# A diffusion trunk's gated linear attention: scan levels grown from the level below, and half of the gate slabs computed with the input

## What is computed

```python
def gla_project(h, w_in, w_a1, w_a2, b_a):
    p = h @ w_in                      # q 512, k 512, v 1024, g 1024 columns
    ...
    low = jnp.einsum('btd,zdr->zbtr', h, w_a1)
    logits = jnp.einsum('zbtr,zrk->zbtk', low, w_a2) + b_a[:, None, None, :]
    log_decay = jax.nn.log_sigmoid(logits.astype(jnp.float32)) / GLA_GATE_NORM
    ...
def step(state, inp):                 # one chunk of tokens, one head
    qc, kc, vc, lc = inp
    cum = jnp.cumsum(lc, axis=2)
    rel = jnp.where(lower, cum[:, :, :, None, :] - cum[:, :, None, :, :], -jnp.inf)
    attn = jnp.einsum('bhtd,bhsd,bhtsd->bhts', qc, kc, jnp.exp(rel))
    last = cum[:, :, -1:, :]
    out = attn @ vc + jnp.einsum('bhtd,bhdv->bhtv', qc * jnp.exp(cum), state)
    state = (jnp.exp(last[:, :, 0, :, None]) * state
             + jnp.einsum('bhsd,bhsv->bhdv', kc * jnp.exp(last - cum), vc))
    return state, out
def gla_output(o, g, head_norm, w_out):
    o = from_heads(rms_norm(o, head_norm))
    return (o * jax.nn.silu(g)) @ w_out
```

## Time and profile before

| | us |
|---|---|
| median of 3 runs | 1734.85 (1732.74 to 1736.03) |
| the profiled execution, its own time | 1732.71 |
| its span, first to last instruction | 1730.9 |
| PE busy | 1661.2 (96%) |
| DVE busy | 1122.6 (65%) |
| ACT busy | 713.6 (41%) |
| POOL busy | 85.8 (5%) |

### The profile page before, as it was taken

The page is one execution under the profiler, slowest core; times in us unless marked ns, Lnnn a source line. Parts: engine busy times, 40 slices in busy tenths (PEclk is TensorE's granted clock), DMA queues, the critical chain, the costliest instruction groups (busy, mean ns, idle before and its releaser), DMA issues.

```text
span 1730.9 us, 23892 instructions
## 1 busy us (share of the span) xinstructions
PE 1661.2 (96%) x9008; PEld 1390.0 (80%) x9008; DVE 1122.6 (65%) x1816; ACT 713.6 (41%) x1060; POOL 85.8 (5%) x57
## 2 busy tenths in 40 slices
PE   7999999998999999999999899989989899999997
PEld 6888877887888888888888777866777688888885
DVE  6678666477877477865775555188855664464456
ACT  4222565336333233322334664256644543343345
POOL 0200000122000000000002200000002100000002
PEclk9999999999999999999999999999999999999999
DMA  8334100031434333334312121110112223333332
GB/s 359 121 141 160 48 1 1 25 134 37 147 101 142 134 109 131 112 134 136 119 62 76 37 64 59 36 35 25 37 62 86 72 94 96 96 95 97 96 97 73
DMA packets 37280, 159.51 MB, mean 92 GB/s; under 512 B 4145, under 2 KB 4401, under 8 KB 31057
## 3 DMA queue, kind: packets, MB, share of 16 engines
q1 hardware_dynamic: 37202, 158.44, 27.5%
HBM read 156.33 MB, written 2.10 MB: 92 GB/s over the span
## 4 chain that ended last, share of the span: by engine, by line
PE 84%; DVE 7%; ACT 5%; issue 2%; DMA 1%; POOL 0%; SPq 0%; ACTq 0%; DVEq 0%
PE pm L484 59%; PE pm L466 5%; PE pm L718 4%; PE pm L638 3%; PE pm L504 2%; PE pm L664 2%; PE pm L897 2%; PE pm L651 1%; ACT mod_t L983 1%; DMA ada_w<-first_ada 1%; DVE h_res L1658 1%; PE pm L840 1%; PE pm L595 1%; PE pm L551 1%; PE pm L822 1%
## 5 line engine op out<-in xcount | busy, mean ns | idle before, releaser
L1382 DVE TENSOR_TENSOR w_lo<-raw,w_hi 128x1024 fp32r<-128x1024 f32 x185 | 230.8, 1249 | 367.0 <-ACT w_hi L964 364.5
L964 ACT ACTIVATE w_hi<-raw 128x1024 fp32r<-128x1024 f32 x181 | 191.8, 1060 | 631.2 <-PE pm L484 535.0
L484 PE MATMUL pm<-x_hi,w_hi 128*128 128x512 f32 (+1 forms) x1464 | 428.8, 354 | 0.7 <-DVE w_lo L1382 0.7
L484 PE MATMUL pm<-x_hi,w_lo 128*128 128x512 f32 (+1 forms) x1464 | 424.0, 351 | 0.0
L484 PE MATMUL pm<-x_lo,w_hi 128*128 128x512 f32 (+1 forms) x1464 | 423.4, 350 | 0.0
L484 PEld LDWEIGHTS pm<-x_lo,w_hi 128*128 128x128 f32 x1464 | 237.8, 189 | 40.6
L484 PEld LDWEIGHTS pm<-x_hi,w_hi 128*128 128x128 f32 x1464 | 237.1, 189 | 39.5 <-issue 1.0
L484 PEld LDWEIGHTS pm<-x_hi,w_lo 128*128 128x128 f32 x1464 | 235.6, 188 | 39.0
L1408 DVE CUSTOM_DVE_ANT_0 ada_w<-ada_w,cond_rep 128x1024 f32<-128x1024 f32 x80 | 102.6, 1282 | 0.0
L484 PE MATMUL pm<-hid_hi,w_hi 128*128 128x512 f32 x330 | 100.6, 359 | 0.2 <-DVE w_lo L1382 0.2
L484 PE MATMUL pm<-hid_lo,w_hi 128*128 128x512 f32 x330 | 99.3, 355 | 0.0
(11 more groups left out here) (242 smaller groups left out, 2525.9 us busy)
## 6 DMA issues: line engine op xcount, KB each, us to landing
raw<-slabs SPq DMA_DIRECT2D x185, 512.0 KB, 3.6
ada_w<-ada SPq DMA_DIRECT2D x44, 1024.0 KB, 4.9
ada_w<-first_ada SPq DMA_DIRECT2D x4, 1024.0 KB, 19.0
raw<-gates SPq DMA_DIRECT2D x8, 512.0 KB, 3.6
h_res<-x SPq DMA_DIRECT2D x4, 768.0 KB, 17.0
out<-h_res SPq DMA_DIRECT2D x8, 256.0 KB, 2.0
rope<-rope SPq DMA_DIRECT2D x1, 512.0 KB, 23.2
level_f<-level SPq DMA_DIRECT2D x1, 448.0 KB, 3.3
```

The lines of the kernel that those rows point to most:

```text
L484: last = pe.matmul(out_p[:, a:b], w[slot][:, ks], x[:, k, a:b], start=(k == 0 and w is w_hi and x is hi), stop=(k == tiles - 1 and w is w_lo))
L964: act.activation(w_hi[nxt % 2][:, :], raw[nxt % 4][:, :], ACT.Copy).then_inc(sem["split_hi"], 1)
L1382: dve.tensor_tensor(w_lo[nxt % 2][:, :], raw[nxt % 4][:, :], w_hi[nxt % 2][:, :].bitcast(FP32), ALU.subtract).then_inc(sem["split_lo"], 1)
```

## The change

1. **Levels grown.** VectorE's step_raw(h) takes the differences of cum from token to token, ScalarE's step_decay(h) their exponential: fold0. GpSimd, which had nothing in the scan, multiplies neighbours: fold1 to fold6, the decay over blocks of 2 to 64 tokens. Keys and queries then grow from level to level: what is faded to its block's middle is multiplied by the neighbouring block's factor, 512 of 1,024 elements each (grow_keys, grow_queries on VectorE, in place in the tile faded). ScalarE's merge_keys copies both halves of the keys into key_sides, which has two buffers; the queries are read by TensorE from faded itself, by an access pattern. Level 1 needs only set_queries. The last factor gives the queries for the states (fade_queries, keep_queries) in place of an exponential per direction.
2. **Gates.** Four slabs of g (the even ones) become ordinary split slabs between the queries and the values (S_GLA_G, take_gate); the other four stay in the scan, one per head, with a new GATE_STEPS: one tile on most steps.
3. **Order in the input.** The last pair of logits and decays goes behind slab 8 instead of 7, for n in (0, 2, 4, 7). The decay exponentials of the chunk sums go ahead of the value slabs.
4. SP waits for q_done as well before it loads over the folds' buffer. The sums of the two directions change places in cum.

The core of the diff:

```diff
         GATE_STEPS = {}
         for h in range(GLA_HEADS):
-            spans = ((0, 3), (3, 6), (6, 8), (8, 11), (11, 13), (13, 15), (15, 16)) if h < GLA_HEADS - 1 else (
-                (0, 4), (4, 8), (8, 11), (11, 14), (14, 16))
-            for b, (k, end) in enumerate(spans):
-                i = 2 * h + k // KT
-                GATE_STEPS[GLA_LEVELS * h + b] = (i, k % KT, (end - 1) % KT + 1)
+            ends = (4, 5, 5, 6, 6, 7, 8) if h == 0 else (2, 3, 4, 5, 6, 7, 8) if h < GLA_HEADS - 1 else (2, 4, 6, 7, 8)
+            for b, (k, end) in enumerate(zip((0,) + ends, ends)):
+                GATE_STEPS[GLA_LEVELS * h + b] = (h, k, end)
...
+        def key_side(h, lv, c):
+
+            if lv <= 1:
+                return gla_k[:, h, c * P:(c + 1) * P]
+            return key_sides[:, lv % 2, c * P:(c + 1) * P]
+
+        def query_side(h, lv, c):
+
+            if lv == 0:
+                return gla_q[:, h, c * P:(c + 1) * P]
+            m = 1 << lv - 1
+            v = faded[:, 0, c * P:(c + 1) * P]
+            return bass.AP(v.tensor, v.offset, [v.ap[0], [2 * m, P // (2 * m)], [3 * LAT + m, 2], [1, m]])
...
-        def segments(b, z, h, src=None):
+        def growing(b, slots, right):
 
             m = 1 << b
-            v = (cum[:, z, h, 0:LAT] if src is None else src).rearrange("p (n t) -> p n t", t=2 * m)
-            mid = m - 1 if z == 0 else m
-            return v[:, :, 0:m], v[:, :, m:2 * m], v[:, :, mid:mid + 1].to_broadcast([P, LAT // (2 * m), m])
+            first, apart = slots
+            v = faded[:, first, :]
+            w = folds[b][:, 0, :]
+            n = LAT >> b
+            blocks, other = [2 * m, n // 2], 1 - 2 * right
+            return (bass.AP(v.tensor, v.offset + m * right, [v.ap[0], [apart * LAT + m * other, 2], blocks, [1, m]]),
+                    bass.AP(w.tensor, w.offset + 1 - right, [w.ap[0], [n - other, 2], [2, n // 2], [0, m]]))
...
-            for i in range(2, KT):
+            for i in range(2, GLA_HEADS):
                 gate_load(i)
             for u in range(2):
-                sp.wait_ge(sem["gate_done"], KT - 1 + u)
+                sp.wait_ge(sem["gate_done"], GLA_HEADS - 1 + u)
                 slab_load(S_GLA_OUT + u, 1 + u)
 
             sp.wait_ge(sem["gram_done"], LEVELS * GLA_HEADS)
             slab_load(S_GLA_OUT + 2, 3)
             sp.wait_ge(sem["s_prod"], 2 * GLA_HEADS)
+            sp.wait_ge(sem["q_done"], GLA_HEADS)
...
-                if n % 2 == 0:
-                    logits(n)
-                    logits(n + 1)
+                if n in (0, 2, 4, 7):
+                    logits(n // 2 * 2)
+                    logits(n // 2 * 2 + 1)
+            for u in range(GLA_HEADS):
+                slab(S_GLA_G, 0, u, x_hi, x_lo, LAT)
...
-                if lv > 0:
-                    m = GLA_LEVELS * h + lv - 1
-                    pe.wait_ge(sem["sides_done"], m + 1)
-                    keys, queries = sides(m)[:, 0, :], sides(m)[:, 1, :]
-                else:
-                    keys, queries = gla_k[:, h, :], gla_q[:, h, :]
+                if lv == 1:
+                    pe.wait_ge(sem["q_set"], h + 1)
+                if lv > 1:
+                    pe.wait_ge(sem["q_grown"], (GLA_LEVELS - 1) * h + lv - 1)
+                    pe.wait_ge(sem["k_merged"], (GLA_LEVELS - 1) * h + lv - 1)
                 for c in range(4):
                     cs = slice(c * P, (c + 1) * P)
-                    last = pe.matmul(level_bank(n)[:, cs], keys[:, cs], queries[:, cs], start=True, stop=True)
+                    last = pe.matmul(level_bank(n)[:, cs], key_side(h, lv, c), query_side(h, lv, c), start=True, stop=True)
                 last.then_inc(sem["gram_done"], 1)
...
-                if n % 2 == 0:
+                if n in (0, 2, 4, 7):
                     softplus(n // 2)
+
+            def take_gate(s, i, u, src):
+                act.activation(gla_g[:, 1, u, :], src[:, 0:LAT], ACT.Copy).then_inc(sem["psum_free"], 1)
+
+            for u in range(GLA_HEADS):
+                step(S_GLA_G, 0, u, take_gate)
             act.wait_ge(sem["ld_done"], 2 * GLA_HEADS)
...
             act.wait_ge(sem["decay_done"], 2)
+            for i in range(2):
...
+            def step_decay(h):
+
+                act.wait_ge(sem["step_raw"], h + 1)
+                act.activation(fold0[:, :, :], fold0[:, :, :], ACT.Exp, scale=INV).then_inc(sem["step_exp"], 1)
+
+            step_decay(0)
...
+            def set_keys(h):
+                if h == 0:
+                    act.wait_ge(sem["x_sum"], KT // 2)
+                else:
+                    act.wait_ge(sem["k_merged"], (GLA_LEVELS - 1) * h)
+                act.activation(faded[:, 1:3, :], gla_k[:, h:h + 1, 0:LAT].to_broadcast([P, 2, LAT]), ACT.Copy).then_inc(
...
+            def merge_keys(h, b):
+
+                n = (GLA_LEVELS - 1) * h + b
+                act.wait_ge(sem["k_grown"], n + 1)
+                if n >= 2:
+                    act.wait_ge(sem["gram_done"], LEVELS * ((n - 2) // (GLA_LEVELS - 1)) + (n - 2) % (GLA_LEVELS - 1) + 3)
+                elif n == 0:
+                    act.wait_ge(sem["x_sum"], KT)
+                m = 2 << b
+                for right in range(2):
+                    part = slice(m * right, m * right + m)
+                    to, own = (v.rearrange("p (n t) -> p n t", t=2 * m)[:, :, part]
+                               for v in (key_sides[:, b % 2, :], faded[:, 2 - right, :]))
+                    last = act.activation(to, own, ACT.Copy)
+                last.then_inc(sem["k_merged"], 1)
+
+            def keep_queries(h):
+
+                act.wait_ge(sem["q_grown"], (GLA_LEVELS - 1) * (h + 1))
                 if h >= 1:
...
+                act.activation(*two_queries(True), ACT.Copy).then_inc(sem["q_kept"], 1)
...
-                    level_decay(GLA_LEVELS * h + b + 2)
+                    if b < GLA_LEVELS - 1:
+                        merge_keys(h, b)
...
+                    if b == 5 and h + 1 < GLA_HEADS:
+                        step_decay(h + 1)
+                    if b == GLA_LEVELS - 1:
+                        keep_queries(h)
+                        if h + 1 < GLA_HEADS:
+                            set_keys(h + 1)
...
-                    decays(n)
-                    decays(n + 1)
+                if n in (0, 2, 4, 7):
+                    decays(n // 2 * 2)
+                    decays(n // 2 * 2 + 1)
+            for u in range(GLA_HEADS):
+                step(S_GLA_G, 0, u)
             for n in range(KT - 2):
                 step(S_GLA_V, n // 4, n % 4)
 
@@ -1779,34 +1841,65 @@
...
+            for h in range(GLA_HEADS):
+                for b in range(1, GLA_LEVELS):
...
+                    two = folds[b - 1][:, :, :].rearrange("p s (n t) -> p s n t", t=2)
+                    pool.tensor_tensor(folds[b][:, :, :].unsqueeze(3), two[:, :, :, 0:1], two[:, :, :, 1:2], ALU.mult).then_inc(
+                        sem["folded"], 1)
```

204 lines of the change are left out of this document (116 added, 88 removed).

## The result

The changed kernel takes 1748.62 us median of 20 runs, before 1736.73 us in the same set: slower by 11.9 us; the ratio over the fast runs is 1.0081, 95% interval 1.006 to 1.0101 (two runs of before took 7523 and 6543 us; without them its median is 1736.1). The profiled execution has a span of 1746.6 us against 1730.9, 15.7 us more. The third pair of gate logits starts at 1034.22 us before and at 1033.81 after, but over all the traces at 1022.0 to 1034.2, though no edit changes TensorE's work ahead of it. So traces are compared here from there on.

The account below looks back on a forecast made before the run. TensorE, busy 96% of the span, was taken as the bound, with VectorE filling head 0 of the scan. Input +30.8, scan -22.4 and folds +3.2 gave +11.6 on 1732.71, so 1744 us; range 1735 to 1750.5.

Parts of the forecast that it names:

- the case of the forecast: Whole kernel: the prediction's own outcome, slower at 1739 to 1749 us, given a chance of 0.60.
- the input's two gaps: TensorE idle 5.3 us before slab 8 and 5.6 us before the third gate slab, each followed by 1.7 us clock loss.
- The input, +30.8: GLA input stage: four added gate slabs (+21.8 us), two waits and clock loss, less an old wait, sum to +30.8 us.
- The scan with the folds, -22.4 and +3.2: Scan of four heads: 114.4 us for 136.85, so -22.4; GpSimd's folds holding up VectorE add 3.2 us.
- the walk's waits: Scan, head by head: TensorE's waits, mostly for grown queries, put at 5.0, 4.0, 2.7 and 3.2 us.
- The strided queries, kept at nothing: Level 1's product reading single elements: nothing in the sum; as rival, doubled time adds 3.6 us, giving 1748; chance 0.10.
- Folds, 2 us in head 0: Start of head 0: GpSimd's folds beside set_queries and the joins cost 2 us, with 0.4 in each other head.
- TensorE's scan closes up: Rival on the scan: product and tile hide the growing, scan -33.2 us, 1730.3 in all; decides at 104 to 105; chance 0.10.

Follow-up runs that it names:

- e5: The kernel before, run again without an edit for a second trace; stages sum to 257.6 us, for 252.9 in its first trace.
- e6: Changed kernel with level 1's product reading the faded queries in a row, so computing other pairs; scan 118.5 us for 119.4.
- e7: Changed kernel with GpSimd's folds of head 0 held back until the last x_sum; head 0 is 0.2 us shorter.
- e12: Changed kernel with sums behind slab 7, gate slabs behind values, step_raw earlier, last head's tiles spread, fade_keys earlier, last output begun early; 1732.07 us for before's 1735.41.
- e13: All edits together on the changed kernel, plus ScalarE's first two output splits later and head 0's tiles spread; 1729.46 us for before's 1734.56.
- e1: Kernel before with the grown levels alone, gate slabs and input order as before; 1733.8 us for 1733.47, ratio 1.0004.
- e2: Kernel before with the moved gate slabs and new input order alone, levels computed as before; 1757.26 us, ratio 1.0147.
- e10: Changed kernel with VectorE's first fade_keys moved up behind the fifth x_sum; head 0 takes 27.33 us for 28.21.

## Where the prediction failed, and why the rest was right

The direction was right, 1748.6 lies in 1735 to 1750.5, and the case of the forecast was the one that came. The predicted 1744 was 4.6 us low.

- **The step that failed: half clock in the scan and behind it was put at nothing, and the sum was laid on "the profiled execution's 1732.71 us", with "so I don't round up".** The prediction counted half clock only behind the input's two gaps, and left it out of the scan and of the stretch behind it without a reason. In the changed kernel's trace it stands behind the first transposes (some 1.5 us, an estimate from the starts of the same instructions in head 1), in the last head's level 7 (0.9) and behind the scan (15.59 us for 13.10, so 2.5). The execution that the sum was laid on had none at the end of the scan and behind it; e5, the same kernel, had 3.3 us there. Against that one execution the stages give +16.1 us for the +11.6 predicted: input 0.4, scan 1.7 and behind the scan 2.5 us more than the sum. Nor is 1732.71 what the kernel takes at its median, 1734.85 then and 1736.73 in the larger set (1736.1 without its two slowest). Laid on these, the same +11.6 gives 1748.3 or 1747.7, against 1748.62 measured. That agreement is in part luck: against e5 the input is +29.8 and the scan -18.4, each about a microsecond off, one each way, and behind the scan there is no difference.

- **The input, +30.8.** Right: +31.2 by the trace. Both gaps stand where they were put. The first is 5.22 us for 5.3, with half clock behind it. The second shows as 3.62 us, since the clock fell also within the slabs ahead of it (0.87 over 1060.3 to 1073.5); its end, 1079.43, is set by VectorE either way, and half clock follows it again (1080.5 to 1083.5). In e6 and e7, without the half clock in the slabs between, the second wait was 5.2 us, and VectorE's 19.2 us from the logits to its end were the same: what half clock costs ahead of a longer wait is absorbed. Their inputs took 136.3 and 136.2 us for 134.0, since the half clock behind each of the two gaps lasted longer (12 to 13 records of 128x512 for 7).
- **The scan with the folds, -22.4 and +3.2.** It gave -17.5. Cut as in the earlier trace rows the heads are 29.1, 31.6, 31.0 and 27.6 us, for 28.4, 31.6, 31.0 and 26.6 with the folds. Heads 1 and 2 are right, though their waits were smaller and level 1 dearer than assumed; the waits before levels 5 to 7 of heads 1 and 2 were 0.6, 0.6 and 1.1 for 0.8, 0.8 and 1.5. TensorE's idle time came to 14.7 us, where the walk's waits add to 14.9; what came out longer is its busy time, 104.7 us for 99.5, with the half clock and the dearer level 1 in it. The 1.7 us missing are in heads 0 and 3, the two with a clock below 1.00, by 0.7 and 1.0 us. In head 3 level 7's product took 2.05 us for the 1.13 of e12. In head 0 some of it is a slip of the prediction: its own four waits there, 1.6, 0.9, 2.1 and 1.5, add to 5.5 us after the 0.15 taken off each, and it wrote 5.0.
- **The strided queries, kept at nothing.** The product costs 0.3 to 0.4 us more, by e6, under half of the doubling that the rival took. In the scan 0.3 to 0.4 us of it showed in all (0.8 us less the 0.5 of level 7's clock). The Trainium skill (Advanced Engine Details and Errata, SBUF Cachelines) asks for two hits on a cacheline and says that there is a penalty otherwise; the sign agrees, with 332 ns a record for 275.
- **Folds, 2 us in head 0.** VectorE lost 1.6 us there (0.85 on set_queries, 0.75 on the joins); e7 shows that it can't be moved away by waiting, but only onto something else.
- **TensorE's scan closes up.** Rightly low: TensorE idles 14.7 us of 119.4. e13 brings it to 9.7 of 113.2, still 9 us off the point at which that rival decides.
- **What was argued on the levels.** The prediction put VectorE's relief and the moved tiles in one walk. e1 and e2 show that this was needed: apart they give +0.3 and +23.8 us by the medians, and a sum of effects taken alone would have been 12 us off.

Open: why the same waits, of 1.97 and 2.74 us, cost half clock in one execution and not in another; where the 12 us ahead of the third pair of logits come from; and what of e10's block of VectorE could go.
